# Sample queries' latent attention: divided by head group, interleaved with the last units of the prompt loop, buffers laid out anew

## What is computed

```python
def _mla_attention(q_lat, q_pe, c_kv, k_pe, q_chunk, k_chunk):
    def blk(qc, qs):
        ql, qp = qs
        logits = (jnp.einsum('bqhc,bkc->bhqk', ql, c_kv, preferred_element_type=jnp.float32)
                  + jnp.einsum('bqhr,bkr->bhqk', qp, k_pe, preferred_element_type=jnp.float32)) * MLA_SCALE
        p = _masked_softmax(logits, qc, k_chunk)
        return jnp.einsum('bhqk,bkc->bqhc', p.astype(c_kv.dtype), c_kv)
    return _sweep_query_blocks(blk, q_chunk, (q_lat, q_pe))
...
    o_lat = _mla_attention(q_lat, q_pe, ckv_all, kpe_all, q_chunk, k_chunk)
    o_b = jnp.einsum('bshc,chv->bshv', o_lat, w_uv)
    o = jnp.concatenate([o_a.reshape(b, s, W_A), o_b.reshape(b, s, W_B)], axis=-1) * jax.nn.silu(gate)
```

## Time and profile before

| | us |
|---|---|
| median of 3 runs | 2057.33 (2054.09 to 2057.75) |
| the profiled execution | 2055.34 |
| span in the profile | 2053.6 |
| PE busy | 1842.7 (90%) |
| DVE busy | 1257.0 (61%) |
| ACT busy | 413.7 (20%) |
| POOL busy | 198.1 (10%) |
| units of the last pair without items, until the sample stage | 913 to 946.7 |
| sample stage | 946.7 to 988.2 |

### The profile page before, as it was taken

How to read it: one execution, slowest core, us unless ns; L and a number is a source line. 1 busy time by engine, 2 the same in 40 slices (tenths; PEclk the granted TensorE clock), 3 DMA queues, 4 the chain that set the end, 5 groups by cost and what they waited for, 6 DMA issues and landing times.

```text
span 2053.6 us, 32706 instructions
## 1 busy us (share of the span) xinstructions
PE 1842.7 (90%) x13182; PEld 1702.1 (83%) x13182; DVE 1257.0 (61%) x1601; ACT 413.7 (20%) x914; POOL 198.1 (10%) x117
## 2 busy tenths in 40 slices
PE   4548999999999999997888889959999999999995
PEld 0108999999999997776777779958999999999995
DVE  4898766776876674553555544377777544574444
ACT  1241000000010113331455533440000000121111
POOL 2770000000600000000000011200000000001110
PEclk8878999999999999999799998979999999999997
DMA  9664554554655532205333253304455332552222
GB/s 387 233 225 175 203 208 185 206 210 185 234 192 211 193 135 62 75 15 164 99 117 117 87 207 128 96 37 169 182 185 202 118 113 103 179 186 82 82 82 87
DMA packets 86106, 316.07 MB, mean 154 GB/s; under 512 B 12184, under 2 KB 20552, under 8 KB 60448
## 3 DMA queue, kind: packets, MB, share of 16 engines
q1 hardware_dynamic: 64208, 237.70, 32.0%
q10 hardware_dynamic: 21200, 76.48, 10.4%
q0 software_dynamic: 640, 1.10, 0.2%
HBM read 282.56 MB, written 32.69 MB: 154 GB/s over the span
## 4 chain that ended last, share of the span: by engine, by line
PE 69%; DVE 12%; DMA 6%; issue 5%; ACT 4%; POOL 2%; SPq 0%; DVEq 0%; ACTq 0%; POOLq 0%
PE banks L732 68%; DVE banks L1645 3%; DMA w_raw<-in_w_pin 3%; POOL ssq L690 2%; DMA w_adr<-in_w_ada_dve 2%; DMA w_more<-in_w_ada_pe 2%; ACT pxd L1428 1%; DVE std L1884 1%; DVE w_hi L1607 1%; DVE h_lo L400 1%; DVE rstd L1587 1%; DVE x L2083 1%; ACT px L1346 0%; DVE pt_lo L1818 0%; DVE w_hi L1868 0%
## 5 line engine op out<-in xcount | busy, mean ns | idle before, releaser
L732 PE MATMUL banks<-h_hi,w_hi 128*128 128x272 f32 x3968 | 831.4, 295 | 61.2 <-DVE w_lo L1608 29.6
L732 PE MATMUL banks<-h_lo,w_hi 128*128 128x272 f32 x3712 | 778.3, 292 | 0.0
L732 PE MATMUL banks<-h_hi,w_lo 128*128 128x272 f32 x3456 | 722.8, 291 | 0.0
L732 PEld LDWEIGHTS banks<-h_hi,w_hi 128*128 128x128 f32 x3968 | 635.4, 194 | 70.3 <-issue 47.8
L732 PEld LDWEIGHTS banks<-h_lo,w_hi 128*128 128x128 f32 x3712 | 596.5, 193 | 0.0
L732 PEld LDWEIGHTS banks<-h_hi,w_lo 128*128 128x128 f32 x3456 | 547.6, 192 | 0.0
L1645 DVE CUSTOM_DVE_ANT_0 banks<-w_adr,cond_b 128x2048 f32<-128x2048 f32 x160 | 386.2, 2414 | 20.2 <-DMA w_adr<-in_w_ada_dve 17.0
L1607 DVE CAST w_hi<-w_raw 128x2048 fp32r<-128x2048 f32 x101 | 125.6, 1244 | 223.4 <-PE banks L732 171.5
L1608 DVE TENSOR_TENSOR w_lo<-w_raw,w_hi 128x2048 fp32r<-128x2048 f32 x101 | 249.2, 2467 | 3.5
L1280 ACT ACTIVATE stage<-banks 128x544 f32<-128x544 f32 x46 | 28.9, 629 | 495.6 <-PE banks L732 495.6
L1976 DVE TENSOR_TENSOR x<-x,stage 128x544 f32 (+1 forms) x32 | 23.9, 748 | 171.0 <-ACT stage L1510 171.0
(11 more groups left out here) (301 smaller groups left out, 1703.8 us busy)
## 6 DMA issues: line engine op xcount, KB each, us to landing
w_adr<-in_w_ada_dve ACTq DMA_DIRECT2D x46, 1024.0 KB, 4.9
w_adr<-in_w_ada_dve SPq DMA_DIRECT2D x34, 1024.0 KB, 4.9
w_raw<-in_w_z SPq DMA_DIRECT2D x32, 1024.0 KB, 5.9
w_raw<-in_w_pin SPq DMA_DIRECT2D x32, 1024.0 KB, 5.9
w_raw<-in_w_gate SPq DMA_DIRECT2D x16, 1024.0 KB, 7.0
w_raw<-in_w_out SPq DMA_DIRECT2D x32, 512.0 KB, 3.9
w_raw<-in_w_pout SPq DMA_DIRECT2D x16, 1024.0 KB, 4.9
w_more<-in_w_ada_pe SPq DMA_DIRECT2D x10, 1024.0 KB, 7.4
```

The costliest lines, as they stand in the source:

```text
L732: return pe.matmul(out, lhsT, rhs, start=start, stop=stop)
```

## The change

The number of instructions and their shapes stay the same, apart from waits. What moves:

- PE's sample work goes into the steps of the unit loop: `samp_keys` at the end of w = 24; scores, turn and values of group 0 at the ends of w = 25, 26, 27; of group 1 at the ends of w = 28, 29, 30; `samp_out` (the `wva` products) at the end of w = 32, ahead of `turn(31)` and `values(7)`. Groups take turns in the same banks, 2 and 3, where before each had its own. DVE's and ACT's parts stand in the step behind, DVE's maximum ahead of `pt_lo`, its normalisation behind the unit's.
- The gate product (`ofs`) and the two halves of h stay behind `finish(7)`.
- Loads: `ccT` goes out as soon as the last item is done, no longer behind `load_sg(3)`; `kpc` and `ccR` behind `ml_score` 24; `wva` and `sgs` behind `ml_pv` 6 (`values(5)`), then `load_sg(3)`. The loads of the differential stage stay behind `ml_fin` 9. The first two halves into `w_raw` also wait for `samp_out`, since `wva` now lies over the even pairs' keys and values, which is the place of `w_raw`.
- New semaphores `ms_mm`, `ms_act`, `ms_vec` count the sample steps of PE, ACT and DVE.

```diff
@@ -146,6 +146,9 @@
         vb_hi0 = sb("vb_hi0", [P, QT, 2 * P], F32R, over_raw)
         vb_lo0 = sb("vb_lo0", [P, QT, 2 * P], F32R, over_raw)
         over_raw.close()
+        over_val = ExitStack()
+        wva = sb("wva", [P, LT, HEADS * P], scope=over_val)
+        over_val.close()
...
@@ -261,17 +264,16 @@
         sb("under_samp", [P, LT * R + (LT * HEADS + HEADS) * NS + 2 * R], scope=ml_samp)
         ccT = sb("ccT", [P, LT, PAST], scope=ml_samp)
         sb("after_ccT", [P, LT * R - LT * PAST], scope=ml_samp)
+        sb("under_units", [P, 20 * NP], scope=ml_samp)
+        ccR = sb("ccR", [P, LT, LORA], scope=ml_samp)
+        kpc = sb("kpc", [P, PAST], scope=ml_samp)
+        ckR = sb("ckR", [P, LORA], scope=ml_samp)
+        pxs = sb("pxs", [P, 2, SKEYS], scope=ml_samp)
         pts = sb("pts", [P, 2, KTS, P], scope=ml_samp)
+        ols = sb("ols", [P, LT, HEADS, NS], scope=ml_samp)
         sgs = sb("sgs", [P, HEADS, NS], scope=ml_samp)
         ofs = sb("ofs", [P, HEADS, NS], scope=ml_samp)
         sts = sb("sts", [P, 2, 4], scope=ml_samp)
-        sb("after_sts", [P, 4 * NP - 2 * KTS * P - 2 * HEADS * NS - 8 + 16 * NP], scope=ml_samp)
-        ccR = sb("ccR", [P, LT, LORA], scope=ml_samp)
-        kpc = sb("kpc", [P, PAST], scope=ml_samp)
-        wva = sb("wva", [P, LT, HEADS * P], scope=ml_samp)
-        ckR = sb("ckR", [P, LORA], scope=ml_samp)
-        pxs = sb("pxs", [P, 2, SKEYS], scope=ml_samp)
-        ols = sb("ols", [P, LT, HEADS, NS], scope=ml_samp)
...
@@ -546,20 +551,22 @@
                     for s in range(2):
                         sp.wait_ge(stored[s], 16 * (ZT + GT) // 2)
                     load_sg(0)
-            for t in range(2, HEADS // 2):
-                sp.wait_ge(ml_fin, 2 * t + 1)
-                load_sg(t)
+            sp.wait_ge(ml_fin, 5)
+            load_sg(2)
             sp.wait_ge(ml_item, ITEMS * (HEADS // 2))
-            sp.wait_ge(ml_score, ML_UNITS - 7)
             sp.dma_start(ccT[:], ckvT.rearrange("(c p) k -> p c k", p=P)).then_inc(ms_in, 16)
-            sp.dma_start(ccR[:], ckv.rearrange("(k p) c -> p k c", p=P)).then_inc(ms_in, 16)
+            sp.wait_ge(ml_score, ML_UNITS - 8)
             for e in range(2):
                 sp.dma_start(kpc[64 * e:64 * e + 64, :], kpeT).then_inc(ms_in, 16)
+            sp.dma_start(ccR[:], ckv.rearrange("(k p) c -> p k c", p=P)).then_inc(ms_in, 16)
+            sp.wait_ge(ml_pv, HEADS - 2)
             for h in range(HEADS):
                 sp.dma_start(wva[:, :, h * P:(h + 1) * P],
                              w_uv[h].rearrange("p (c v) -> p c v", c=LT)).then_inc(ms_w_in, 16)
+            sp.dma_start(sgs[:], g_scr[HEADS:2 * HEADS, :, NP:R].rearrange("h p r -> p h r")).then_inc(ms_w_in, 16)
+            sp.wait_ge(ml_fin, 7)
+            load_sg(3)
             sp.wait_ge(ml_fin, HEADS + 1)
-            sp.dma_start(sgs[:], g_scr[HEADS:2 * HEADS, :, NP:R].rearrange("h p r -> p h r")).then_inc(ms_w_in, 16)
 
             def load_head(h):
                 s = h % 2
@@ -591,6 +598,7 @@
                     sp.wait_ge(x1_out[n % 2], 16 * (n // 2))
                 sp.dma_start(x_half[n % 2][:], xT[:, n]).then_inc(x1_in[n % 2], 16)
 
+            sp.wait_ge(ms_mm, S_OUT)
             for n in range(2):
                 load_half(w_out[n][:, D // 2:D], G_OUT + n)
             sp.wait_ge(ms_fin, 1)
@@ -915,6 +923,53 @@
...
+            def samp_keys():
+                pe.wait_ge(ml_ev, ITEMS * (HEADS // 2))
+                for c in range(LT):
+                    m = pe.transpose(PS[0:NS, 3, c * P:(c + 1) * P], ckT[:, c, NP:R], id_t[:])
+                m.then_inc(ms_mm, 1)
+
+            def samp_scores(g):
+                if g == 0:
+                    pe.wait_ge(ms_in, 64)
+                pe.wait_ge(ms_act, S_VALUE_EV[0] if g else S_KEYS_EV)
...
+            def samp_turn(g):
+                pe.wait_ge(ms_vec, S_NORM[g])
...
+            def samp_values(g):
+                pe.wait_ge(ms_vec, S_TURN_EV[g])
...
+            def samp_out():
+                pe.wait_ge(ms_act, S_VALUE_EV[1])
+                pe.wait_ge(ms_w_in, 16 * (HEADS + 1))
+                for h in range(HEADS):
...
@@ -932,48 +987,19 @@
                 if w < ML_UNITS - 8:
                     for k in items_at[w % 8]:
                         item(w // 8 + 1, k)
-
+                if w == ML_UNITS - 8:
+                    samp_keys()
+                for g, w0 in enumerate((ML_UNITS - 7, ML_UNITS - 4)):
+                    if w == w0:
+                        samp_scores(g)
+                    if w == w0 + 1:
+                        samp_turn(g)
+                    if w == w0 + 2:
+                        samp_values(g)
+                if w == ML_UNITS:
+                    samp_out()
 
             pe.wait_ge(ml_fin, HEADS + 1)
-            for c in range(LT):
-                m = pe.transpose(PS[0:NS, 4, c * P:(c + 1) * P], ckT[:, c, NP:R], id_t[:])
...
-                m.then_inc(ml_score, 1)
-            for g in range(2):
-                pe.wait_ge(ml_norm, ML_UNITS + g + 1)
-                pe.wait_ge(mq_ev, 1)
...
-            pe.wait_ge(ms_olev, 2)
-            pe.wait_ge(ms_w_in, 16 * (HEADS + 1))
...
             pe.wait_ge(ms_fin, 1)
@@ -1355,19 +1381,21 @@
                 if w < ML_UNITS - 8:
                     for k in items_at[w % 8]:
                         item_hi(w // 8 + 1, k)
+                if w == ML_UNITS - 8:
+                    act.wait_ge(ms_mm, S_KEYS)
+                    act.activation(ckR[0:NS, :], PS[0:NS, 3, :], ACT.Copy).then_inc(ms_act, 1)
+                for g, w0 in enumerate((ML_UNITS - 7, ML_UNITS - 4)):
+                    if w == w0 + 1:
+                        act.wait_ge(ms_vec, S_MAX[g])
+                        act.activation(rows(pxs[:, g]), PS[:, 2:4, 0:HALF], ACT.Exp, bias=sts[:, g, 1:2],
+                                       scale=MLA_SCALE, accum_out=sts[:, g, 2:3]).then_inc(ms_act, 1)
+                    if w == w0 + 3:
+                        act.wait_ge(ms_mm, S_VALUE[g])
+                        act.activation(ols[:, :, 4 * g:4 * g + 4, :].rearrange("p c h r -> p c (h r)"),
+                                       PS[:, 2, :].rearrange("p (c n) -> p c n", c=LT), ACT.Copy).then_inc(ms_act, 1)
                 if w >= LAG + 4 and (w - LAG) % 4 == 0:
                     out_hi((w - LAG) // 4 - 1)
 
-            act.wait_ge(mq_tr, 1)
-            act.activation(ckR[0:NS, :], PS[0:NS, 4, :], ACT.Copy).then_inc(mq_ev, 1)
...
@@ -1811,6 +1839,15 @@
                     dve.wait_ge(ml_score, w + 1)
                     vchain(dve, dve.tensor_reduce(st[:, 0, w:w + 1], PS[:, w % 2, 0:n], AX.X, ALU.max))
                     dve.tensor_scalar(st[:, 1, w:w + 1], st[:, 0, w:w + 1], -MLA_SCALE, None, ALU.mult).then_inc(ml_max, 1)
+                for g, w0 in enumerate((ML_UNITS - 7, ML_UNITS - 4)):
+                    if w == w0 + 1:
+                        dve.wait_ge(ms_mm, S_SCORE[g])
+                        vchain(dve, dve.tensor_reduce(sts[:, g, 0:1], PS[:, 2:4, 0:HALF], AX.XY, ALU.max))
+                        dve.tensor_scalar(sts[:, g, 1:2], sts[:, g, 0:1], -MLA_SCALE, None, ALU.mult).then_inc(ms_vec, 1)
+                    if w == w0 + 2:
+                        dve.wait_ge(ms_mm, S_TURN[g])
+                        dve.tensor_copy(pts[:, g, 0:KTS - 1, :].rearrange("p j q -> p (j q)"), PS[:, 2, :])
+                        dve.tensor_copy(pts[0:NS, g, KTS - 1, :], PS[0:NS, 3, 0:P]).then_inc(ms_vec, 1)
                 if LAG <= w < ML_UNITS + LAG:
                     v = w - LAG
                     s, i = unit(v % 8)
@@ -1823,6 +1860,11 @@
                     vchain(dve, dve.reciprocal(st[:, 3, w:w + 1], st[:, 2, w:w + 1]))
                     dve.tensor_scalar(px[:, w % 3, 0:n], px[:, w % 3, 0:n], st[:, 3, w:w + 1], None,
                                       ALU.mult).then_inc(ml_norm, 1)
+                for g, w0 in enumerate((ML_UNITS - 7, ML_UNITS - 4)):
+                    if w == w0 + 1:
+                        dve.wait_ge(ms_act, S_EXP[g])
+                        vchain(dve, dve.reciprocal(sts[:, g, 3:4], sts[:, g, 2:3]))
+                        dve.tensor_scalar(pxs[:, g], pxs[:, g], sts[:, g, 3:4], None, ALU.mult).then_inc(ms_vec, 1)
                 if w < ML_UNITS - 8:
                     for k in items_at[w % 8]:
                         item_out(w // 8 + 1, k)
@@ -1836,20 +1878,9 @@
                 dve.tensor_tensor(lo, src, hi.bitcast(F32), ALU.subtract).then_inc(done, 1)
 
 
-            for g in range(2):
-                dve.wait_ge(ml_score, ML_UNITS + g + 1)
-                vchain(dve, dve.tensor_reduce(sts[:, g, 0:1], PS[:, 2 * g:2 * g + 2, 0:HALF], AX.XY, ALU.max))
-                dve.tensor_scalar(sts[:, g, 1:2], sts[:, g, 0:1], -MLA_SCALE, None, ALU.mult).then_inc(ml_max, 1)
-            for g in range(2):
-                dve.wait_ge(ml_exp, ML_UNITS + g + 1)
```

(59 more changed lines are left out.)

37 lines of the change are left out of this document (1 added, 36 removed).

## The result

The changed kernel takes 2069.77 us in the median of 4 runs (2067.35 to 2071.37), the kernel before in the same comparison 2055.71. The ratio is 1.0068, 95% interval 1.0051 to 1.0086: 14 us slower, between 10 and 18. The forecast was 2068 us, 11.2 slower. In a second comparison the ratio was 1.0069 (1.0054 to 1.0084).

What follows compares the result with a forecast made beforehand. PE bounds the kernel (69% of the chain), the sample stage being a serial relay. ml_fin = 9 at 989.1 plus 14.0 puts the first latent product at 1003.1, 11.2 us later: 2068 us, range 2056.5 to 2075.

Steps and rivals of the forecast that it cites:

- The bound and the method: Sample stage is a serial relay with PE idle beside units; three queues walked at 2.4 GHz, 7.8 us short before.
- Part 1: Ahead of the first sample scores, PE waits for all four early loads: 6.6 us (4.8 to 9.3).
- the sum: Added work, waits and low-clock time up to ml_fin = 9, put at 989.1; whole kernel 2068 us.
- Part 2: Interleaved sample stretch: 1.2 GHz adds 5.2 (wva products), 1.8 (values(7)) and some 1.7 (first scores), together 8.7 us.
- rival E: Group scores and values: PE's stalls inside the steps keep the clock low there too, 6.6 us more, 2074.5; chance 0.11.
- Part 3: Start of the differential stage: its loads lose their cover and 9.1 us are exposed (5.7 to 11).
- B: Interleaved stretch: a filled PE stays at 2.4 GHz; first latent product at 994.4, +2.5, 2060 us; chance 0.09.
- C: Differential stage absorbs its late start: the 9.1 us vanish, +2.1 stays, 2059.5 us; chance 0.08.
- D: Sample and differential stages: clock stays up and no load is exposed; -6.6 us, 2050.7; chance 0.06.

Runs made afterwards that it cites:

- the first experiment: Kernel before, with the differential stage's loads issued only when the wva products are done; ratio 1.0041 (1.0028 to 1.0053), 8.4 us slower.

## Why the prediction was right, point by point

**The bound and the method.** Right. The walk through three queues, checked first on the kernel before, gave the waits of the new order to within 0.4 us each: predicted 1.2, 1.6, 2.7, 3.9 and 1.6 in steps 26, 27, 28, 29 and 31, and 1.0 before values(7); measured 1.26, 1.53, 2.38, 3.52, 1.42 and 0.69.

**Part 1, the wait for the loads.** Right: 6.6 predicted, 6.48 measured. That it is so near is partly luck: the loads took 9.0 us from the issue of ccT to the start of the scores (911.93 to 920.97; 8.4 in the sum, whose bytes of 924 to 931 also hold those of wva, issued from 926.02 on the earlier trace rows), and PE came to the wait 0.7 us later than in the sum. Taken away with its low-clock tail it gave back 8 us (6.6 + 1.7 predicted), with some 4 us of uncertainty. The tail is in the windows of the changed kernel. PE stood still from 914.5 to 920.97. The clock fell within that (1.00 until 918, 0.57 on average in 918 to 922), and it took until past 925 to come back, with PE busy all the time from 920.97 on:

```profile
915.00:918.00 3.00, 0.00 (x0) 0.00 (x0) 1.26 (x6) 0.73 (x3) 0.00 (x0) 1.00 1.05 371
918.00:922.00 4.00, 1.03 (x2) 0.84 (x3) 0.00 (x0) 0.00 (x0) 0.00 (x0) 0.57 0.57 216
922.00:925.00 3.00, 3.00 (x8) 2.26 (x7) 0.00 (x0) 0.00 (x0) 0.00 (x0) 0.50 0.00 0
925.00:928.00 3.00, 3.00 (x17) 2.72 (x16) 0.00 (x0) 0.00 (x0) 0.00 (x0) 0.93 0.00 0
...
955.00:960.00 5.00, 2.18 (x11) 2.03 (x11) 2.19 (x7) 1.60 (x5) 0.00 (x0) 0.61 0.00 0
960.00:965.00 5.00, 5.00 (x28) 4.59 (x27) 3.17 (x8) 1.33 (x4) 0.00 (x0) 0.71 0.00 0
...
975.00:980.00 5.00, 5.00 (x25) 5.00 (x25) 0.00 (x0) 0.00 (x0) 0.00 (x0) 0.50 0.00 0
```

**Part 2, the clock terms.** Mechanism right, size short: this is the term that was mis-sized. From the last item to ml_fin = 9 the sum had 78.0 us; the profiled execution took 82.6. Of the 4.6, 2.4 are in the rows from 955 to 965 above: behind the wait of step 29 the turn, scores(30) and part of values(6) ran at 1.2 GHz (5.98 us from 957.82 to 963.80, 3.62 in the second profile, at full clock). Of rival E, which put this at 6.6 us, a third came true. Another 0.6 lie in the wva products (13.35 for 12.7) and 0.5 in the first scores. The rest, about 1, is no clock: the units' own scores and turns from step 26 on take 9.5 us in the timeline at full clock where the sum has 8.0, PE reaches the first wait 0.7 later, and the waits in the steps are together 10.8 and not 12.0. (The scores of a group were also put at 5.35 where 10.80 / 2 is 5.40, 0.1 us in all.) How far this term depends on the execution is shown by the second profile of the very same kernel, where the windows from 955 to 970 are at 1.00 and the wva products take 11.28 (the windows from 955 to 965):

```profile
955.00:960.00 5.00, 2.20 (x17) 2.09 (x18) 2.81 (x10) 1.58 (x5) 0.00 (x0) 1.00 0.00 0
960.00:965.00 5.00, 5.00 (x36) 4.45 (x35) 3.12 (x7) 1.69 (x4) 0.00 (x0) 1.00 0.00 0
```

There the first latent product comes 91.3 us after the last item; the sum had 92.0, and the first profile 95.5. So the sum lies between two executions of the kernel, and the nearness of the total (11.2 us predicted, 14 measured) is partly two errors against each other: up to ml_fin = 9 the sum was 4.6 us short in the first profile, and the exposed loads were put 1.2 us too large.

**Part 3, the exposed loads.** Right: predicted 9.1, measured 8.4 in the kernel before (6 to 11), 7.9 between the two traces (11.6 less 3.7). The details: w_out halves issued 4.0 us behind ml_fin = 9 (4.1), landed in 6.5 (7.3). They are the last of ten loads in one queue; alone in it they took 3.8 in the run with samp_out last, near the median over the span, 3.9. The sum did not name vds, for which PE waits first (10.10 us); it lands early enough that the halves still decide, by 1.07 us.

**Rivals.** B (the clock stays) is out: 0.50 from 975 to 990. The Trainium skill (TensorE: Matmul & The Clock Gate, Part 1: The HAM clock gate) names activity as what releases the throttle. The rows do not bear out the reading "busy is enough": PE was busy 5.00 of 5 us with both forms of the wva products, and the granted clock was 0.50 with 128 stationary and 32 moving columns, 1.00 with 32 and 128. C (absorption) is out by the first experiment. D had no case left without B and C.

**What the change was worth by itself.** The interleaving was a gain in the end, of 5 us, once nothing it uncovered was left open; the expectation, from PE's idle time beside the units, was nearly twice that. That relay waits and low clock kept the rest is read from the trace of that version and was not tried by itself.

## What to carry to other kernels

Before a stage is moved into the gaps of another, list what that stage was covering. Here it was 36 us of cover for ten loads, and the stage's own loads had theirs from the units; the move cost both, some 16 us in all (8 and 8.4). The whole change cost 14, so the interleaving gave back 2 to 3. Free the buffers so that each load can be issued a stage ahead, give loads that are wanted later a semaphore of their own, and check each queue for what stands in front of the load that is wanted first.
